# Prompt attention of a streaming encoder step: the two heads of a pair computed side by side, and a longer pipeline between the engines

## The reference

```python
qg = qb.reshape(B, blk, N_KV_HEADS, N_GROUPS, HEAD_DIM)      # 4 key-value heads, 4 query heads on each, 64 wide
logits = jnp.einsum('btkgd,btskd->btkgs', qg, kg) * scale
logits = jnp.where(valid[:, :, None, None, :], logits, -jnp.inf)
p = jax.nn.softmax(logits, axis=-1)
o = jnp.einsum('btkgs,btskd->btkgd', p, vg)
...
out = o @ w_out            # added to x
```

## Time and profile before

| | |
|---|---|
| median of 3 runs | 4009.2 us (4008.99 to 4009.93) |
| profiled execution | 4001.8 us, span 4000.2 us |
| granted TensorE clock over the span | 0.892 |
| PE busy | 3700.2 us (93%), 19764 instructions |
| PEld busy | 3266.8 us (82%) |
| DVE busy | 2125.7 us (53%) |
| ACT busy | 1185.8 us (30%) |
| POOL busy | 229.3 us (6%) |

### The profile page before, as it was taken

One profiled execution on the slowest core, in us unless ns is written; L12 is line 12 of the kernel. 1 busy time (PEld: TensorE's weight loads), 2 busy tenths in 40 slices (PEclk: granted clock), 3 DMA queues, 4 the chain that ended last, 5 costly groups with the idle time before them and its releaser, 6 DMA issues. The chain is left out here.

```text
span 4000.2 us, 55681 instructions
## 1 busy us (share of the span) xinstructions
PE 3700.2 (93%) x19764; PEld 3266.8 (82%) x19780; DVE 2125.7 (53%) x3935; ACT 1185.8 (30%) x1961; POOL 229.3 (6%) x349
## 2 busy tenths in 40 slices
PE   6999999998999999999789869997889999999997
PEld 5989898896999999998537835654448899999997
DVE  5456555555545555556787745333223555455556
ACT  4223223333111111114357654444332311111112
POOL 2000000001000000002000011000001000000001
PEclk8888888887999999999679956678999999999998
DMA  2111010110111111112011220002321111111111
GB/s 85 33 38 38 28 38 28 38 38 19 48 38 43 48 38 43 48 41 84 11 64 65 75 80 11 6 1 91 139 115 53 35 43 48 38 43 49 38 43 60
DMA packets 57408, 192.24 MB, mean 48 GB/s; under 512 B 7016, under 2 KB 23408, under 8 KB 52528
## 3 DMA queue, kind: packets, MB, share of 16 engines
q1 hardware_dynamic: 52992, 167.89, 12.3%
q0 software_dynamic: 4144, 20.71, 1.4%
HBM read 166.64 MB, written 21.93 MB: 47 GB/s over the span
## 5 line engine op out<-in xcount | busy, mean ns | idle before, releaser
L292 PE MATMUL ff1lin<-ff1h_hi,ff1w_hi 128*128 128x384 f32 x1056 | 354.8, 336 | 9.3 <-DVE ff1w_lo L286 5.7
L292 PE MATMUL ff0lin<-ff0h_hi,ff0w_hi 128*128 128x384 f32 x1056 | 354.1, 335 | 7.2 <-DVE ff0w_lo L286 4.4
L294 PE MATMUL ff1lin<-ff1h_hi,ff1w_lo 128*128 128x384 f32 x1056 | 353.8, 335 | 0.0
L293 PE MATMUL ff1lin<-ff1h_lo,ff1w_hi 128*128 128x384 f32 x1056 | 353.7, 335 | 0.0
L294 PE MATMUL ff0lin<-ff0h_hi,ff0w_lo 128*128 128x384 f32 x1056 | 353.3, 335 | 0.0
L293 PE MATMUL ff0lin<-ff0h_lo,ff0w_hi 128*128 128x384 f32 x1056 | 353.3, 335 | 0.0
L292 PE MATMUL hg_lin<-hg_h_hi,hg_w_hi 128*128 128x384 f32 x768 | 270.6, 352 | 16.2 <-POOL hg_h_lo L165 14.2
L293 PE MATMUL hg_lin<-hg_h_lo,hg_w_hi 128*128 128x384 f32 x768 | 264.5, 344 | 0.0
L294 PE MATMUL hg_lin<-hg_h_hi,hg_w_lo 128*128 128x384 f32 x768 | 264.2, 344 | 0.0
L2227 DVE CUSTOM_DVE_ANT_0 ap_probs<-ap_bank,mask_p 128x512 f32<-128x512 f32 (+3 forms) x192 | 101.9, 556 | 229.4 <-PE ap_bank L2105 214.1
L292 PEld LDWEIGHTS ff1lin<-ff1h_hi,ff1w_hi 128*128 128x128 f32 x1056 | 199.0, 188 | 12.2 <-DVE ff1w_lo L286 6.3
(11 more groups left out here) (429 smaller groups left out, 8205.3 us busy)
## 6 DMA issues: line engine op xcount, KB each, us to landing
ff_raw<-in_weights SPq DMA_DIRECT2D x132, 512.0 KB, 3.5
hg_raw<-in_weights SPq DMA_DIRECT2D x40, 512.0 KB, 3.5
as_keys<-in_cache_k SPq DMA_DIRECT2D x16, 1024.0 KB, 4.9
as_vals<-in_cache_v SPq DMA_DIRECT2D x8, 2048.0 KB, 9.2
se_keys<-in_cache_ki SPq DMA_DIRECT2D x8, 1024.0 KB, 4.9
pb_raw<-in_weights SPq DMA_DIRECT2D x12, 512.0 KB, 3.5
x<-in_x SPq DMA_DIRECT2D x3, 1536.0 KB, 9.5
x_keep<-x POOLq DMA_DIRECT2D x1, 4608.0 KB, 18.4
```

The costliest lines, as they stand in the source:

```text
L292: pe.matmul(out, w_hi, x_hi, start=start, stop=False)
L293: pe.matmul(out, w_hi, x_lo, start=False, stop=False)
L294: return pe.matmul(out, w_lo, x_hi, start=False, stop=stop)
```

## The change

- A score step computes one piece of up to 512 keys for both halves, with the three matmuls of the halves alternating. The banks alternate by piece instead of holding the two pieces of a half, so a step waits for the reads of the piece two before (`qk_read`), not for a maximum.
- Transposes are counted by bank (`turn_pieces`), and PE's step starts with them; the scores stand behind.
- ACT's exponential is one step later (block n - 1), so that scores, exponential and transposes are of three successive blocks.
- A group's value products move from the end of its last block to behind the first scores of two steps later, in one burst as before; `probs_t` gets a second buffer so that the next group's copies need not wait. It lies where `x` lies, so the reload of `x` moves to the end of SP's queue in `attend_sample_phase`.
- The inverse of the sums is spread over the four steps behind its group.

```diff
+    probs, probs_t = take("ap_probs", [P, 2, 2, T_PROMPT]), take("ap_probs_t0", [P, PT, 2, COLS])
+    probs_t = probs_t, take("ap_probs_t1", [P, PT, 2, COLS], at=t_at["x"])
...
-                if t == 1:
-                    sp.dma_start(x[:, :, :], io["x_keep"]).then_inc(x_back, 16)
...
-            def scores(n, half):
+            def scores(n, c):
                 t, j = blocks[n]
-                rows = slice(half * HEAD_D, (half + 1) * HEAD_D)
+                k, a, e = score_pieces[n][c]
                 pe.wait_ge(q_lo_set, n + 1)
-                if n:
-                    pe.wait_ge(maxed, 2 * n + half - 1)
-                for c, (a, e) in enumerate(pieces((t + 1) * P)):
-                    out, keys = qk[half][c][:, 0:e - a], (rows, j // GROUP, slice(a, e))
-                    pe.matmul(out, q_hi[rows, j, :], k_hi[keys], start=True, stop=False)
-                    pe.matmul(out, q_lo[rows, j, :], k_hi[keys], start=False, stop=False)
-                    i = pe.matmul(out, q_hi[rows, j, :], k_lo[keys], start=False, stop=True)
+                if k >= 2:
+                    pe.wait_ge(qk_read, 2 * (k - 1))
+                outs = [qk[half][k % 2][:, 0:e - a] for half in range(2)]
+                rows = [slice(half * HEAD_D, (half + 1) * HEAD_D) for half in range(2)]
+                keys = (j // GROUP, slice(a, e))
+                for half in range(2):
+                    pe.matmul(outs[half], q_hi[rows[half], j, :], k_hi[(rows[half], *keys)], start=True, stop=False)
+                for half in range(2):
+                    pe.matmul(outs[half], q_lo[rows[half], j, :], k_hi[(rows[half], *keys)], start=False, stop=False)
+                for half in range(2):
+                    i = pe.matmul(outs[half], q_hi[rows[half], j, :], k_lo[(rows[half], *keys)], start=False, stop=True)
                 i.then_inc(qk_done, 1)
...
+                for k, a, e in turn_pieces[2 * n + half]:
+                    if k >= 2:
+                        pe.wait_ge(turned_out, k - 1)
+                    for c in range(a // P, e // P):
+                        i = pe.transpose(tr[k % 2][:, c * P - a:(c + 1) * P - a], probs[:, n % 2, half, c * P:(c + 1) * P],
+                                         const["ident"][:, :])
+                    i.then_inc(turned, 1)
...
+                if part == 0:
+                    pe.wait_ge(turned_out, turns_up_to(GROUP * u + GROUP - 1, 1))
+                    pe.wait_ge(o_set, u)
+                for c in value_parts(t, part):
...
-                    if n < len(blocks):
-                        scores(n, half)
                     if 0 <= m < len(blocks):
                         turn(m, half)
-                if m > 0 and m % GROUP == 0:
-                    spread_sums(m // GROUP - 1)
-                if 0 <= m < len(blocks) and m % GROUP == GROUP - 1:
-                    values(m // GROUP)
+                    if half == 0 and m >= GROUP and m % GROUP == 0:
+                        turn_inv(m // GROUP - 1)
+                    if half == 1 and m > GROUP and m % GROUP == 1:
+                        spread_sums(m // GROUP - 1)
+                    if n < len(blocks) and half < len(score_pieces[n]):
+                        scores(n, half)
+                    if m >= GROUP:
+                        values(m // GROUP - 1, 2 * (m % GROUP) + half)
...
+                            act.activation(probs_t[u % 2][:, a // P:b // P, half, cols], tr[k % 2][:, 0:b - a].rearrange("p (c t) -> p c t", t=P),
+                                           ACT.Copy).then_inc(turned_out, 1)
...
+                    if 0 <= e < len(blocks):
...
+                        act.wait_ge(maxed, 2 * e + half + 1)
...
+                k, a, e = score_pieces[n][c]
+                last = c == len(score_pieces[n]) - 1
+                dve.wait_ge(qk_done, k + 1)
+                for half in range(2):
+                    if n >= 2:
+                        dve.wait_ge(turned, turns_up_to(n - 2, half, min(c, len(score_pieces[n - 2]) - 1)))
+                    dve.tensor_tensor_reduce(out=probs[:, n % 2, half, a:e], in0=qk[half][k % 2][:, 0:e - a],
...
+            sp.dma_start(x[:, :, :], io["x_keep"]).then_inc(x_back, 16)
+            sp.wait_ge(x_back, 16)
```

More of the change, by code:

```diff
@@ L2034, in attend_prompt_phase @@
     k_lo = take("ap_k_lo", [P, 2, T], F32R, at=t_at["at_k"])
-    part_max, neg_max = take("ap_part_max", [P, 2, 2]), take("ap_neg_max", [P, 2, 2, 1])
+    part_max, neg_max = take("ap_part_max", [P, 2, 2, 2]), take("ap_neg_max", [P, 2, 2, 1])
     total, inv = take("ap_total", [P, 2, 2 * GROUP]), take("ap_inv", [P, 2, 2 * GROUP])
@@ L2043, in attend_prompt_phase, with scores_up_to, turns_up_to, value_parts @@
     groups = [(t, p) for t in range(PT) for p in range(2)]
-    LAG, AHEAD = 2, QB - 2
+    LAG, TAIL, AHEAD = 2, GROUP, QB - 2
+    score_pieces, turn_pieces = [], []
+    for t, j in blocks:
+        at = sum(len(p) for p in score_pieces)
+        score_pieces.append([(at + c, a, e) for c, (a, e) in enumerate(pieces((t + 1) * P))])
+        for half in range(2):
+            at = sum(len(p) for p in turn_pieces)
+            turn_pieces.append([(at + c, a, e) for c, (a, e) in enumerate(pieces((t + 1) * P))])
+    def scores_up_to(n):
+        return score_pieces[n][-1][0] + 1
+    def turns_up_to(n, half, c=-1):
+        return turn_pieces[2 * n + half][c][0] + 1
+    def value_parts(t, part):
+        return [c for c in range(t + 1) if 0 == part]
     SIGN_STEP, first_sample = 3, env["sample_steps"]
@@ L2097, in scores @@
                 i.then_inc(qk_done, 1)
             def turn(n, half):
-                t, j = blocks[n]
                 pe.wait_ge(exped, 2 * n + half + 1)
[L2102 to L2107, removed]
@@ L2113, in values, with turn_inv @@
+            def turn_inv(u):
                 pe.wait_ge(inv_set, u + 1)
@@ L2115, in values @@
                 pe.transpose(ib[0:2 * GROUP, 0:P], inv[:, u % 2], const["ident"][:, :]).then_inc(inv_turned, 1)
-                pe.wait_ge(turned_out, 2 * GROUP * (u + 1))
-                pe.wait_ge(o_set, u)
-                for c in range(t + 1):
+            def values(u, part):
+                t, p = groups[u]
+                if part == 0:
+                    pe.wait_ge(turned_out, turns_up_to(GROUP * u + GROUP - 1, 1))
+                    pe.wait_ge(o_set, u)
+                for c in value_parts(t, part):
                     for half in range(2):
                         col = (p * 2 + half) * HEAD_D
-                        i = pe.matmul(ob[half * HEAD_D:(half + 1) * HEAD_D, :], v_sb[:, c, col:col + HEAD_D], probs_t[:, c, half, :],
-                                      start=c == 0, stop=c == t)
-                i.then_inc(pv_done, 1)
+                        i = pe.matmul(ob[half * HEAD_D:(half + 1) * HEAD_D, :], v_sb[:, c, col:col + HEAD_D],
+                                      probs_t[u % 2][:, c, half, :], start=c == 0, stop=c == t)
+                    if c == t:
+                        i.then_inc(pv_done, 1)
             def spread_sums(u):
+                if u == 0:
+                    pe.wait_ge(consts_in, 32)
                 pe.wait_ge(inv_rows_set, u + 1)
@@ L2178, in _ @@
                         r = half * GROUP + j % GROUP
-                        act.activation(probs[:, n % 2, half, 0:keys], probs[:, n % 2, half, 0:keys], ACT.Exp, bias=neg_max[:, n % 2, half],
+                        act.activation(probs[:, e % 2, half, 0:keys], probs[:, e % 2, half, 0:keys], ACT.Exp, bias=neg_max[:, e % 2, half],
                                        accum_out=total[:, u % 2, r:r + 1]).then_inc(exped, 1)
```

75 lines of the change are left out of this document (31 added, 44 removed).

## The result

The changed kernel takes 3849.2 us (median of 4 runs, 3848.6 to 3851.0) against 4009.1 for the kernel before, a ratio of 0.961 (95% interval 0.9589 to 0.963). The forecast was 3885 and its range began at 3860: the direction was right, the gain larger. Part of that is the kernel before, which varies: a fourth run took 3995.6 us, and its medians further down are 3994 to 4002. The profiled execution took 3848.9 us, 152.9 less than that of before. 143.9 of them lie in the stage, which shrank from 454.2 us (first score to last output) to 310.3. Another 8.3 lie ahead of it, in phases with the same code. Behind the stage nothing changed (0.7).

The account below looks back on a forecast made before the run. PE bounds the prompt attention from tile 2, a chain between engines tiles 0 and 1. 174 + 132 + 23.6 = 330 us replace 454.3, 125 less: median 3885 us, own range 3855 to 3910, 8-in-10 range 3860 to 3950.

Parts of the forecast that it names:

- Scores side by side: Score matmuls of the two halves overlap fully; a pair in tile 7 falls from 5.22 to 3.86 us of PE.
- The clock: Tiles 4 to 6: granted clock above 0.9; PE's 208 us assumes the upper level; called the weak term.
- the new order takes the 64-row stretches away: Tiles 5 to 7: clock fell after 64-row scores and transposes; removing 64-row stretches favours the upper level; no size.
- The middle: Tiles 0 to 3: midway between busiest-engine floor and present time or lower-clock PE: 27, 35, 29, 41, together 132 us.
- The 7% for delays between engines: Tiles 4 to 7: 7% added to the larger of PE and ACT, giving 36, 41, 46, 51, 174 us.
- The tail: End of the stage: last copies, values and inverse stay at 23.6 us, work the same.
- Tile 4: PE needs 33.8 us at the upper clock; with 7% on the larger engine the tile takes 36 us.
- The base of the sum: Whole kernel: profile near 3877, median 3885, since the profiled 4001.8 us lay 7 us under the median of 4009.2.
- The exponential's place: Tiles 0 to 3: one exponential's distance more between engines shortens the chain; no row for how far, middle taken.
- The later values: Value products behind the next pair's first scores: only takes away the wait for the last copies; no number.
- The reload of x: Moved to the sample attention's end: lands about 2992, costs nothing with 17 us of cover, up to 16 without.
- Rivals B to E: B: clock keeps falling, 3943, 0.17; C: never rises, 4018, 0.04; D: no overlap, 4009, 0.03; E: engine waits, 3915, 0.12.

## Why the prediction was off, point by point

**Scores side by side: right.** The overlap is full. Without it PE's work grows by 18 us in tiles 5 to 7 (a lower bound, above), and tiles 2 to 4 lose 32 us to work and clock together.

**The clock: right in its outcome, wrong in its reasons.** Tiles 5 to 7 were at 1.00; tile 4, at 0.87, stayed under the 0.9 that the prediction named. But "the new order takes the 64-row stretches away" is not the cause by itself: with every half alone tiles 6 and 7 run at 1.00 as well, once the 8-row matmul is cut and the exponential is late. And "the bursts, which alone lifted it so far" holds for the old order only. What the runs show in its place is that one wait of about 2 us a group was followed by a fall each time that it came at the upper level, and that the old order came back to that level only in a burst. The 8-row matmul beside lone 64-row scores stood ahead of most of the old order's falls, but cutting it gave 23 us, not 64 to 84; why, once it is cut, falls still follow it in tiles 1 to 4 and not in 6 and 7 stays open.

The mechanism was right, then, and the sizes failed, in the stage and outside it.

**"The middle" for tiles 0 to 3: the term that failed by most.** The forecast had 132 us, and it was 119.3: 28.0 in tile 0, and 91.3 in tiles 1 to 3 instead of 105. The upper bound was PE at the lower clock, but tile 2 ran at 1.00 and tile 3 at 0.88. That comes with the overlap and not with the later exponential: tiles 2 and 3 take 84.2 us with the halves apart, 59.9 in the changed kernel and 60.5 with the exponential in its own step. A slip adds to it: by its own bounds (30.6 and 46) the middle of tile 3 is 38, not 41; it took 37.4.

**The 7% for delays between engines: it failed too.** It was taken from a tile with the old waits, which also stood at the lower level for 3.4 us. Measured tiles 5 to 7 are 39.2, 43.2 and 47.5 against PE's sums of 37.7, 42.8 and 47.8: no delay in the last two. That is 8 us too much.

**The tail**, "its work is the same", took 16.3 in place of 23.6: PE had 11.9 us of work left in it instead of 17.1, at a clock of 0.90 instead of 0.70. **Tile 4** went the other way, 44.7 against 36: the search's closing steps, which I had counted for tile 3 only. With all of them in tile 3 it took 34.6. Together these make the 20 us by which the stage came out shorter.

**The base of the sum** gave the other 16 us of the miss. They lie outside the stage: 8.3 ahead of it, and some 8 because I carried the distance of one profile from the median of before over to the changed kernel, where the two are the same. By the stage alone the median would have been 4009.2 less 143.9, or 3865, inside the range; the range had no room for scatter in the other phases and in the kernel before.

**The exponential's place: under-rated.** The prediction gave the later exponential a small gain in tiles 0 to 3. It is worth 142 us in the changed kernel, nearly all in tiles 4 to 7, because without it the new order of the scores stalls ACT. **The later values** were priced as a wait taken away, without a number; putting them back costs 16 us, mostly by a wait for `o_t` that the old order does not have, and taking the second buffer away costs 9. The parts do not add: alone on the kernel before, the exponential gives 23, and the scores without the pipeline lose 23.

**The reload of x:** nothing, as predicted. A small misreading without effect: PE, VectorE and ACT were busy for 50 to 78% of tiles 0 and 1, not 47. Rivals B to E did not come: the level stays up from tile 5 on, the halves overlap, and ACT's loss of a burst stays hidden behind PE.

## What to carry to other kernels

Where a kernel runs at the lower clock with PE nearly always busy, look at what stands just ahead of each fall: here a short wait cost about four times its own length, because the level stayed low long after it. Change the order of one engine's work and the distance to the engines behind it together, and test each part in the finished order too: the later exponential alone gave 23 us less and the new order of the scores alone 23 more, all parts together 144 less. And a delay factor measured under the old waits does not belong in the sum for an order that removes them.

## What the hardware showed unasked

Matmuls in different 64 rows started together even when the code lists one half's three before the other's: the fourth in the list began 10 ns after the first. And a burst of full-array products was not needed for the upper level (0.887 over the stage without bursts, 0.878 with them).
